# Delta rule's side work in its projection, GpSimd's products behind the solve, equal column blocks

## The reference, cut to what matters

```python
# GatedDeltaNet layer of the second block (float32); 1 of 4 layers. d = 128, hq = 4, hv = 8, L = 64
def gdn_mixer(xn, w_in, conv_w, a_log, dt_bias, o_gain, w_out):
    qkv, z, a, b = jnp.split(xn @ w_in, [GDN_CONV_DIM, GDN_CONV_DIM + GDN_WIDTH, GDN_CONV_DIM + GDN_WIDTH + hv], axis=-1)
    qkv = jax.nn.silu(causal_conv(qkv, conv_w))
    q, k, v = jnp.split(qkv, [hq * d, 2 * hq * d], axis=-1)
    q = jnp.repeat(l2_norm(q.reshape(bsz, s, hq, d)), rep, axis=2) * d ** -0.5
    k = jnp.repeat(l2_norm(k.reshape(bsz, s, hq, d)), rep, axis=2)
    beta = jax.nn.sigmoid(b.astype(f32))
    g = -jnp.exp(a_log) * jax.nn.softplus(a.astype(f32) + dt_bias)
    gc = jnp.cumsum(to_chunks(g, L), axis=-1)
    diff = gc[..., :, None] - gc[..., None, :]
    decay = jnp.where(causal, jnp.exp(jnp.where(causal, diff, 0.0)), 0.0)
    tri = jnp.where(strict, jnp.einsum('bhnld,bhnmd->bhnlm', kb, kc) * decay, 0.0) + jnp.eye(L)
    u = triangular_solve(tri, vb)
    w = triangular_solve(tri, kb * jnp.exp(gc)[..., None])
    qk = jnp.einsum('bhnld,bhnmd->bhnlm', qc, kc) * decay
    q_dec = qc * jnp.exp(gc)[..., None]
    k_dec = kc * jnp.exp(g_last[..., None] - gc)[..., None]
    # scan over chunks: v_new = u - w S; o = q_dec S + qk v_new; S = S exp(g_last) + k_dec v_new
    o = rms_norm(o, o_gain).reshape(bsz, s, GDN_WIDTH)
    return (o * jax.nn.silu(z)) @ w_out
...
for layer in range(4):            # fox, gla, gdn, fox
    xn = rms_norm(x, norm_w[layer])
    x = x + mixer(xn, ...)        # widths of w_in: 4104, 3088, 3088, 4104 columns, 1024 rows
```

## Time and profile before

| | |
|---|---|
| time, median of 3 (range) | 1687.67 us (1687.59 to 1692.89) |
| the profiled execution: its own time | 1688.17 us |
| its span | 1686.4 us |
| PE busy | 1530.2 us, 91% of the span |
| DVE, ACT, POOL busy | 872.2 us (52%), 660.3 us (39%), 184.3 us (11%) |
| mean granted TensorE clock | 0.948 of full |
| fox_in0, from its first transposes | 983.4 us |
| gla_in0; gdn_in0; gdn0_prepare | 1143.1; 1286.2; 1380.8 us |
| gdn0_mid; gdn_out0; fox_in1 | 1396.9; 1492.9; 1522.5 us |

### The profile page before, as it was taken

How to read it: one execution, slowest core, us unless ns; L and a number is a source line. 1 busy time by engine, 2 the same in 40 slices (tenths; PEclk the granted TensorE clock), 3 DMA queues, 4 the chain that set the end, 5 groups by cost and what they waited for, 6 DMA issues and landing times. The chain is left out here.

```text
span 1686.4 us, 19232 instructions
## 1 busy us (share of the span) xinstructions
PE 1530.2 (91%) x7648; PEld 1176.7 (70%) x7648; DVE 872.2 (52%) x1160; ACT 660.3 (39%) x890; POOL 184.3 (11%) x102
## 2 busy tenths in 40 slices
PE   6999899989999898888999999889989967889987
PEld 2774669758878574666887768777867754667876
DVE  1756664665544525547553355364444645464634
ACT  1433331344333343434433245534533452235542
POOL 0005440030000200302000001100000004000300
PEclk7999899899999997999999989998998988899999
DMA  8653470556545456146654356315404420016621
GB/s 310 230 171 120 143 282 1 200 175 194 180 137 188 155 171 220 50 127 198 196 178 153 97 175 197 127 52 184 166 29 151 154 72 2 1 51 179 205 91 51
DMA packets 152424, 243.07 MB, mean 144 GB/s; under 512 B 13824, under 2 KB 62924, under 8 KB 151951
## 3 DMA queue, kind: packets, MB, share of 16 engines
q1 hardware_dynamic: 151422, 237.60, 43.7%
q0 software_dynamic: 912, 4.24, 0.7%
HBM read 240.72 MB, written 1.10 MB: 143 GB/s over the span
## 5 line engine op out<-in xcount | busy, mean ns | idle before, releaser
L197 DVE TENSOR_TENSOR w_lo<-w_raw,w_hi 128x2048 fp32r<-128x2048 f32 (+2 forms) x176 | 392.2, 2234 | 299.0 <-ACT w_hi L188 298.5
L220 PE MATMUL ps<-w_hi,act_hi 128*128 128x512 f32 (+3 forms) x1216 | 476.6, 392 | 15.2 <-issue 6.8
L188 ACT CAST w_hi<-w_raw 128x2048 fp32r<-128x2048 f32 (+2 forms) x176 | 316.6, 1804 | 394.1 <-PE ps L222 231.5
L222 PE MATMUL ps<-w_hi,act_lo 128*128 128x512 f32 (+3 forms) x1216 | 469.6, 386 | 0.0
L221 PE MATMUL ps<-w_lo,act_hi 128*128 128x512 f32 (+3 forms) x1216 | 469.3, 386 | 0.0
L220 PEld LDWEIGHTS ps<-w_hi,act_hi 128*128 128x128 f32 x1216 | 234.7, 193 | 70.8 <-issue 12.5
L222 PEld LDWEIGHTS ps<-w_hi,act_lo 128*128 128x128 f32 x1216 | 234.7, 193 | 46.0
L221 PEld LDWEIGHTS ps<-w_lo,act_hi 128*128 128x128 f32 x1216 | 235.0, 193 | 44.9 <-issue 1.2
L204 PE MATMUL ps<-con 128*128 128x512 f32 x218 | 107.7, 640 | 24.3 <-DVE up L3129 18.0
L204 PEld LDWEIGHTS ps<-con 128*128 128x128 f32 x218 | 43.2, 209 | 73.4 <-issue 73.4
L294 PE MATMUL ps<-w_raw,condz 128*32 128x512 f32 x384 | 60.6, 738 | 25.0 <-DMA w_raw<-in_ada_w 15.1
(11 more groups left out here) (483 smaller groups left out, 1841.8 us busy)
## 6 DMA issues: line engine op xcount, KB each, us to landing
w_raw<-in_ada_w SPq DMA_DIRECT2D x48, 1024.0 KB, 6.2
w_raw<-in_ffn_w_in SPq DMA_DIRECT2D x88, 512.0 KB, 4.9
w_raw<-in_fox_w_in SPq DMA_DIRECT2D x32, 1024.0 KB, 7.6
w_raw<-in_ffn_w_out SPq DMA_DIRECT2D x20, 1024.0 KB, 5.0
w_raw<-in_rwkv_w_rkv SPq DMA_DIRECT2D x12, 1024.0 KB, 5.9
w_raw<-in_gla_w_in SPq DMA_DIRECT2D x12, 1024.0 KB, 5.1
w_raw<-in_gdn_w_in SPq DMA_DIRECT2D x12, 1024.0 KB, 5.1
w_raw<-in_fox_w_out SPq DMA_DIRECT2D x8, 1024.0 KB, 5.0
```

The source lines that it names most:

```text
L188: self.nc.scalar.copy(hi[:, s, 0:c["nk"], 0:c["width"]], self.raw[:, c["slot"], 0:c["nk"], 0:c["width"]]).then_inc(self.hi_done, 1)
L197: self.nc.vector.tensor_tensor(lo[:, s, 0:c["nk"], 0:c["width"]], self.raw[:, c["slot"], 0:c["nk"], 0:c["width"]], hi[:, s, 0:c["nk"], 0:c ...
L220: nc.tensor.matmul(out(t)[:, 0:w], xh[:, k, tok], hi[:, s, j, 0:w], start=first, stop=False)
L222: r = nc.tensor.matmul(out(t)[:, 0:w], xl[:, k, tok], hi[:, s, j, 0:w], start=False, stop=last)
```

## The change

1. **Equal blocks.** In fox_in0, gla_in0, gdn_in0 and fox_in1 the first block takes the rest of the columns and the head of the matrix together, and all blocks are equally wide: 9 of 456 for fox; 6 of 448 and 1 of 400 for gla and gdn. Each layer's projection is one tensor `proj`; q, k, v, z, u and the gates are views of it.
2. **gdn_prepare is gone.** Softplus and gate hang behind block 0 and 1, the cumulative sums behind block 2. The differences are no longer built on TensorE: the row of cumulative sums goes to HBM and comes back spread over the partitions (as in fox), GpSimd adds it to the masks (4 instructions), and ScalarE takes exp with the column as its bias (16 instructions of 128x128 behind block 4 for `am`, 16 behind block 5 for `qk`). Squares go behind block 4, sums behind 5, norms behind 6; GpSimd's power and its two products by -beta close its list.
3. **gdn_mid** opens with the transposes of q and k and the grams. GpSimd's `kdec`, second `bv`, `qk` and `z` products wait for the end of the solve (`up_back` 4).
4. `stage_ln` (layer norm ahead of fox_in0) issues 7 `keep_warm` matmuls where it issued 12. gla's gate weights are loaded by GpSimd's queue in place of SyncE's.

```diff
-            core.keep_warm(12)
+            core.keep_warm(7)
...
+    @on("pool", 0)
+    def _(pool, sem):
+        nc.gpsimd.memset(up[0:32, :], 0.0).then_inc(sem("blank"), 1)
+        pool.wait_ge(sem("blank"), 1)
+        nc.gpsimd.dma_start(up[0:16, :], a["gla_w_gate_up_2"][i]).then_inc(sem("up"), 16)
+        nc.gpsimd.dma_start(up[32:33, :], a["gla_b_gate_2"][i:i + 1, :]).then_inc(sem("up"), 16)
 
...
     def back(pe, sem, c):
 
         pe.wait_ge(sem("silu"), c + 1)
+        if c == 0:
+            pe.wait_ge(sem("gc"), 4)
         if c:
             pe.wait_ge(sem("back"), 2 * c)
...
+    def logs(act, sem):
+        act.wait_ge(sem("taken"), NT)
+        nc.scalar.activation(w["beta"][:, :, :], ab[:, :, VH:2 * VH], ACT.Sigmoid).then_inc(sem("beta"), 1)
+        act.wait_ge(sem("vec"), 32)
+        act.wait_ge(sem("a"), 1)
+        nc.scalar.activation(vec[:, 0, :], vec[:, 0, :], ACT.Exp).then_inc(sem("ea"), 1)
+        act.wait_ge(sem("abs"), 1)
+        nc.scalar.activation(sc[:, 1, :, :], sc[:, 1, :, :], ACT.Exp, scale=-1.0).then_inc(sem("e"), 1)
+        act.wait_ge(sem("e"), 1)
+        nc.scalar.activation(sc[:, 1, :, :], sc[:, 1, :, :], ACT.Ln, bias=core.c("ones")[:, 0:1]).then_inc(sem("e"), 1)
+
...
+    def cums(pe, sem):
+        pe.wait_ge(sem("g"), 1)
+        for t in range(NT):
+            nc.tensor.matmul(ps[:, 7, 8 * t:8 * t + 8], core.c("tri"), g[:, t, :], start=True, stop=True)
+            nc.tensor.matmul(ps[:, 7, 16 + 8 * t:24 + 8 * t], core.c("after"), g[:, t, :], start=True, stop=True)
+            r = nc.tensor.matmul(ps[0:VH, 6, t * P:t * P + P], g[:, t, :], core.c("neg_tri"), start=True, stop=True)
+        r.then_inc(sem("cums"), 1)
+
+    def decays(act, sem):
+        act.wait_ge(sem("cums"), 1)
+        nc.scalar.copy(w["nrow"][0:VH, :], ps[0:VH, 6, 0:T]).then_inc(sem("nrow"), 1)
+        nc.scalar.copy(w["gc"][:, :, :], small(0)).then_inc(sem("gc"), 1)
+        nc.scalar.activation(w["ngc"][:, :, :], small(0), ACT.Copy, scale=-1.0).then_inc(sem("gc"), 1)
+        nc.scalar.activation(w["egc"][:, :, :], small(0), ACT.Exp).then_inc(sem("gc"), 1)
+        nc.scalar.activation(w["eaft"][:, :, :], small(16), ACT.Exp).then_inc(sem("gc"), 1)
+
...
+    def spread(pool, sem):
+        add = nc.gpsimd.tensor_tensor
+        pool.wait_ge(sem("nrow"), 1)
+        nc.gpsimd.dma_start(a["gate_rows"], w["nrow"][0:VH, :]).then_inc(sem("row_out"), 16)
+        pool.wait_ge(sem("row_out"), 16)
+        src = bass.AP(tensor=a["gate_rows"].tensor, offset=0, ap=[[0, P], [T, VH], [1, T]])
+        nc.gpsimd.dma_start(rows[:, :, :], src).then_inc(sem("row_in"), 16)
+        pool.wait_ge(sem("row_in"), 16)
+        for t in range(NT):
+            add(am[:, VH * t:VH * t + VH, :], rows[:, :, t * P:t * P + P], bc_out(core.c("strict"), VH), ALU.add).then_inc(sem("row"), 1)
+        for t in range(NT):
+            add(qk[:, VH * t:VH * t + VH, :], rows[:, :, t * P:t * P + P], bc_out(core.c("incl_t"), VH), ALU.subtract).then_inc(sem("row"), 1)
+        pool.wait_ge(sem("qk_ms"), 1)
+        add(st[:, 16:32], st[:, 16:32], core.c("mhalf")[:, 0:16], ALU.pow).then_inc(sem("rn"), 1)
+        for t in range(NT):
+            pool.wait_ge(sem("dec"), VH * t + VH)
+            x = am[:, VH * t:VH * t + VH, :]
+            add(x, x, bc_in(w["nbeta"][:, t, :], P), ALU.mult).then_inc(sem("decay"), 1)
+
+    def exps(turned):
+        def fn(act, sem):
+            if not turned:
+                act.wait_ge(sem("row"), 2)
+            for t in range(NT):
+                act.wait_ge(sem("row"), 2 * turned + t + 1)
+                for h in range(VH):
+                    n = VH * t + h
+                    if turned:
+                        r = nc.scalar.activation(qk[:, n, :], qk[:, n, :], ACT.Exp, scale=-1.0, bias=w["ngc"][:, t, h:h + 1])
+                    else:
+                        r = nc.scalar.activation(am[:, n, :], am[:, n, :], ACT.Exp, bias=w["gc"][:, t, h:h + 1])
+                    r.then_inc(sem("dec_t" if turned else "dec"), 1)
+        return fn
+
+    def squares(act, sem):
+        act.wait_ge(sem("back"), 4)
+        for t in range(NT):
+            nc.scalar.activation(sq[:, t, :], u[:, t, 0:2 * QH * P], ACT.Square).then_inc(sem("sq"), 1)
+
+    def sums(dve, sem):
+        dve.wait_ge(sem("sq"), 2)
+        nc.vector.reduce_sum(st[:, 0:16], sq[:, :, :].rearrange("p i (h j) -> p (i h) j", j=P), axis=AX_X).then_inc(sem("sums"), 1)
+        dve.wait_ge(sem("sums"), 1)
+        nc.vector.tensor_scalar(st[:, 16:32], st[:, 0:16], RMS_EPS, None, ALU.add).then_inc(sem("qk_ms"), 1)
+
...
+    side["sync", 0] = vectors
+    side["pool", 0] = spread
+    also("dve", 0, softplus)
+    also("act", 0, logs)
+    also("dve", 1, gate)
+    before = side["pe", 2]
+    side["pe", 2] = lambda pe, sem: (cums(pe, sem), before(pe, sem))
+    first = side["act", 2]
+    side["act", 2] = lambda act, sem: (decays(act, sem), first(act, sem))
+    also("dve", 3, cut)
+    also("act", 4, squares)
+    also("act", 4, exps(False))
+    also("dve", 5, sums)
+    also("act", 5, exps(True))
...
+            def turn(s, t, bank):
+                for h in range(QH):
+                    c0 = (s * QH + h) * P
+                    r = nc.tensor.transpose(ps[:, bank, h * P:h * P + P], u[:, t, c0:c0 + P], core.c("ident"))
+                r.then_inc(sem("turn"), 1)
...
-            for t in range(NT):
-                diff(t, 0, 2 * t, False)
-                diff(t, 1, 2 * t + 1, False)
+            turn(1, 0, 0)
+            turn(1, 1, 1)
+            turn(0, 0, 2)
+            turn(0, 1, 3)
+            for t in range(NT):
+                pe.wait_ge(sem("turned"), t + 1)
                 gram(t, 4 + t, QH, "kk")
-            diff(0, 0, 6, True)
-            diff(0, 1, 7, True)
-            pe.wait_ge(sem("exp"), 4)
-            diff(1, 0, 0, True)
-            diff(1, 1, 1, True)
-            gram(0, 2, 0, "kq_mm")
-            gram(1, 3, 0, "kq_mm")
+            for t in range(NT):
+                pe.wait_ge(sem("turned"), t + 3)
+                gram(t, 6 + t, 0, "kq_mm")
             pe.wait_ge(sem("kk_used"), 4)
-            pe.wait_ge(sem("exp_t"), 4)
             pe.wait_ge(sem("kq"), 2)
             pe.wait_ge(sem("up_back"), 1)
...
-            for c in range(4):
-                t, b = c // 2, c % 2
-                pool.wait_ge(sem("exp"), c + 1)
-                mul(am[:, 4 * c:4 * c + 4, :], am[:, 4 * c:4 * c + 4, :], bc_in(w["nbeta"][:, t, 4 * b:4 * b + 4], P), ALU.mult).then_inc(sem("decay"), 1)
             nc.gpsimd.memset(up[:, 0:NT * VH, :], 0.0).then_inc(sem("blank"), 1)
             mul(heads(w["bv"][:, 0, :]), heads(u[:, 0, 2 * QH * P:]), bc_in(w["beta"][:, 0, :], P), ALU.mult).then_inc(sem("bv"), 1)
+            pool.wait_ge(sem("up_back"), 4)
             for r in range(2):
                 mul(w["kdec"][:, :, :].rearrange("p (h r) j -> p h r j", r=2)[:, :, r, :], heads(u[:, 0, QH * P:2 * QH * P]),
                     bc_in(w["eaft"][:, 0, :].rearrange("p (h r) -> p h r", r=2)[:, :, r], P), ALU.mult).then_inc(sem("kdec"), 1)
-            for t in range(NT):
-                pool.wait_ge(sem("exp_t"), 2 * t + 2)
+            mul(heads(w["bv"][:, 1, :]), heads(u[:, 1, 2 * QH * P:]), bc_in(w["beta"][:, 1, :], P), ALU.mult).then_inc(sem("bv"), 1)
+            for t in range(NT):
                 pool.wait_ge(sem("kq"), t + 1)
                 for r in range(2):
                     mul(by_pair(qk, t)[:, :, r, :], by_pair(qk, t)[:, :, r, :], heads(mm.kq[:, t, :]), ALU.mult).then_inc(sem("qk"), 1)
-            mul(heads(w["bv"][:, 1, :]), heads(u[:, 1, 2 * QH * P:]), bc_in(w["beta"][:, 1, :], P), ALU.mult).then_inc(sem("bv"), 1)
...
+def in_width(n):
+
+    return -(-n // -(-n // COLS) // 16) * 16 if n % 16 == 0 else -(-n // -(-n // COLS) // 8) * 8
+
+
 def in_blocks(n):
 
-    b = blocks(n)
-    return b[-1:] + b[:-1]
+
+    tail, w = n % COLS, in_width(n)
+    first = [[(n - tail, tail), (0, w - tail)]]
+    return first + [[(at - tail, min(w, n - at))] for at in range(w, n, w)]
 
```

231 lines of the change are left out of this document (88 added, 143 removed).

## The result

The changed kernel takes 1649.97 us (median of 4 runs, 1648.74 to 1652.74) where the kernel before takes 1688.22 in the same comparison: a ratio of 0.977, 95% interval 0.9747 to 0.9793, so 35 to 43 us faster. The profiled execution took 1648.74 us, its span is 1647.0. Forecast was 1640 with a range of 1628 to 1656: the sign and the main parts hold, the gain was 38 instead of 47.5 us.

The account below looks back on a forecast made before the run. TensorE, busy 91% of the span, was taken as the bound, through matmul count, interval and clock. Gains 6.0 + 0.5 + 7.4 + 31.4 + 5.6 = 50.9, less 3.4, gave 47.5 us: 1688.17 to 1640.7, said as 1640, range 1628 to 1656.

Parts of the forecast that it names:

- Equal blocks: Four projections: equal widths remove narrow blocks at low clock; fox_in0 -6.0, gla_in0 -7.4, fox_in1 -5.6 us, before clock drops.
- two starts dropped the clock: Projection starts: a 2.6 us gap ahead of the first matmul drops the clock at two of four, +3.4 us (0 to 6.8).
- stage_ln: Layer norm ahead of fox_in0: five keep_warm fewer at 0.227 us each, -0.5 us (0 to -1.1).
- gdn_in0: Delta rule's projection: stage grows 3 us but gdn0_prepare's 16.1 us goes, -12.8 us before any clock drop.
- The second wait: TensorE's second wait for SiLU in gdn_in0: GpSimd's additions hold conv(1), so it becomes 2.9 us.
- gdn0_mid: Stage with the solve: -9.2 us up to the block transposes and -9.4 in the solve.
- those 7 cost 2.0: Solve in gdn0_mid: 7 of 30 steps, 11.41 us beside GpSimd, cost 2.0 with its products behind the solve: -9.4 us.
- The lock: GpSimd and two-SBUF-operand VectorE work exclude each other: norms and products take turns, 6.5 us; otherwise 2.5 more gain.
- A: Rival: gdn_in0's side work does not fit, exponentials and additions delay splits and taps; stage grows 12 us, kernel 1652; chance 0.11.
- B: Rival: the solve's slow steps are not GpSimd's doing, so the 9.4 us stays; kernel 1650; chance 0.04.
- C: Rival: matmul interval does not follow columns, 448 still takes 227 ns; 40 us lost, 1681, counted as no change; chance 0.03.
- D: Rival: clock stays low after each of four starts, from 26 us on; with 30 us, kernel slower at 1697; chance 0.03.

Follow-up runs that it names:

- e4: Changed kernel with the old blocks again (8 or 16 narrow columns first, then blocks of 512): 1672.60 us.
- e1: Changed kernel with blocks of 464 columns in the four projections: 1647.44 us.
- e2: Changed kernel with blocks of 480 columns in the four projections: 1650.62 us.
- e10: Changed kernel with uneven blocks (first 264 columns in fox, 272 in gla and gdn, then 512, last 256): 1642.30 us.
- e5: Changed kernel with 11 instead of 1 keep_warm calls between transposes and first matmul in all four projections: 1665.97 us (one run).
- e3: Changed kernel with GpSimd's kdec, second bv, qk and z products no longer waiting for the solve's end: 1654.41 us; gdn0_mid 80.12 us.
- e8: Changed kernel with GpSimd's two products by -beta moved to the start of gdn0_mid: 1647.33 us (one run); gdn_in0 101.25 us.
- e7: Changed kernel with am's exponentials moved behind block 5 and qk's into gdn0_mid: 1649.12 us (one run); gdn_in0 98.41 us.

## Why the prediction was right, and by what it was short

**Equal blocks: the mechanism held, one term was mis-sized.** The narrow blocks and their low clock went, the start grew to 5.4 us as worked out (though the cast's 1.79 us is a distance from start to start, not shown in the earlier trace rows, where one takes 1.95), and two starts dropped the clock for 3.4 us each. That it was two is luck: the forecast put a gap at all four starts and had nothing to choose between none and four; there were three gaps, and from run to run one to three of them cost the clock. What failed is "512 columns at 2.4 GHz are 213.3 ns, so the row's 227 leaves 13.4 that I keep fixed". At 456 columns a matmul takes 208.9 ns, not 203, over 432 matmuls 2.5 us in each fox layer, where 2.5 and 2.1 are missing; at 448 it is 202.7, 0.8 us in gla and in gdn each. In gla the 5.1 gained hold 1.7 that the widths did not bring (e4): the sum had taken the first two blocks at the 21.2 us of one trace. The Trainium skill ("TensorE: Matmul & The Clock Gate", section "Wait — 56ns, not 53.3ns?") has 2.5 ns as the fixed cost and would have put the error on the other side; here no width shows less than 11 (e1, e2, e10).

**stage_ln.** -0.3 for -0.5. But the bound rested on 0.227 us a call, and a call is 0.86 (e5): TensorE was relieved of 4.3 us and left idle for as long, and VectorE sets the end. With a call at 0.86 the bound would have been 4.3, so that -0.5 came near (-0.3 here, some -0.6 in the runs of the experiments) is luck. The transposes at the lower clock (3.65 us) were hidden by the wider split, as said, and only by it (e4).

**gdn_in0.** -8.9 for -11.1 (with its drop). Right: first wait 2.75 (2.7), third 4.66 (4.3), norms and products in turns 5.9 and 11.3 us from the last convolution to the end of the norms (11.9). The second wait was 1.32, not 2.9: the additions did hold conv(1), for 6.2 us, but block 4's matmuls covered it. Wrong: no term stood for the clock falling in the waits themselves. Block 4 took 11.1 us instead of 9.8, the transposes behind the waits 0.6 to 0.9 more each, and the exponentials ahead of the third wait cost 0.30 each, not 0.25. So conv(3), from which the last chain hangs, ended 90.2 us after the stage's start (1367.8) and not 87.3 (the 85.6 of the sum and one clock drop); the chain behind it was 0.6 shorter than said, and 2.2 remain. Wrong also, but without weight: the last wait, which I left at 2.30 "as before". It is 3.54, since another table load (1.28) now stands ahead of that SiLU; the transposes behind it end 0.9 us ahead of the norms.

**gdn0_mid: right sum, partly wrong reason.** -18.4 for -18.6. From the start to the block transposes 7.9 us (7.4), the solve 8.65 (8.7), behind it no change. But "with GpSimd's products behind the solve those 7 cost 2.0" credited the whole 9.4 to the wait; e3 shows that 6.9 come from GpSimd's shorter list and 2.5 from the wait. I had priced the state before and the state after, and not the state with one edit alone.

**The lock** of the Trainium skill ("SBUF — State Buffer", section "SBUF: two separate sides") is borne out: the norms take 5.89 us beside two products and 2.50 without them (e8), a step of 0.21 takes 2.28 beside a product (e3), and transposes of 32x32 blocks are not held. It did not turn the sign.

**Rivals.** A (side work does not fit) came in small: ScalarE's eight microseconds did delay block 6, at 3.4 us (e7), not 12. B falls with e3 and the 8.65 us. C: the interval follows the columns, with an extra of 3 to 5 ns at 448 and 456. D: the clock was low for 3.4 us behind a gap, not 26.

Together: fox 4.6 short, gla 0.6, gdn_in0 2.2, layer norm and gdn0_mid 0.4, the stages ahead 1.7, less gla_out0's 1.3: 8.2 us, from 1640.7 to the profiled 1648.7 within 0.2. The last two of these, +1.7 and -1.3, lie in stages that the change does not touch; that they nearly cancel is luck.

## What to carry to other kernels

When a wait or a split of work is lengthened, price what it does to TensorE's clock as well as the time itself: in this program a gap of 2.6 us or a little more ahead of a projection cost another 1.2 to 2.8 us in 18 of 24 cases, and a gap cut to 1.3 us or less cost nothing in nine. Moving GpSimd's work is worth only the part that still overlaps two-operand VectorE work once everything else has moved; try each edit alone. And before equalising block widths, measure the interval at the width that comes out: wide blocks with one of half width at either end were 3 us a fox layer better than nine equal ones, 1.1 to 1.4 of it by the earlier first matmul.

## What the runs showed of the hardware that was not expected

- The cost of an fp32r matmul above its columns' time is 11 to 14 ns at 256 to 400 columns and at 512, but 16.0 at 448, 18.9 at 456, 16.6 at 464 and 16.7 at 480. The cause is open. Below some width the interval no longer falls: 112 ns at 8, 16 and 208 columns (e4, e2).
- (A size of my own, not the chip's.) A `keep_warm` call with float32 operands of 512 columns is two rows of 0.43 us, not one of 0.23.
- Short matmuls of 264 and 272 columns, 120 to 126 ns apart, kept the clock at 1.00 (e10), where those of 8 and 16 let it fall.
- VectorE's 32x32 block transposes took 7.71 us alone and 7.82 beside GpSimd's products; the first four taps, which read one tensor and a column, were held too: 7.47 us beside additions instead of 1.23.
